# Cached key and value products of the sample group as 32-row products on four column quarters

## What is computed

```
s = jnp.einsum('bqhd,bld->bqhl', qi, ki)           # indexer scores, top 256 of 2056 keys
logits = jnp.einsum('bqhd,bqkhd->bqhk', q, ks) * HEAD_DIM ** -0.5
p = softmax(logits over the selected keys)
ya = jnp.einsum('bqhk,bqkhd->bqhd', p, vs)         # 8 heads of 64
```

## Time and profile before

| | us |
|---|---|
| median of 3 runs | 1352.07 |
| the runs | 1347.96, 1352.07, 1356.02 |
| span of the profiled execution | 1348.8 |
| TensorE busy | 1272.5 (94%) |
| VectorE busy | 712.7 (53%) |
| ScalarE busy | 251.3 (19%) |
| mean granted TensorE clock | 0.954 |

### The profile page before, as it was taken

One profiled execution on the slowest core, in us unless ns is written; L12 is line 12 of the kernel. 1 busy time (PEld: TensorE's weight loads), 2 busy tenths in 40 slices (PEclk: granted clock), 3 DMA queues, 4 the chain that ended last, 5 costly groups with the idle time before them and its releaser, 6 DMA issues.

```text
span 1348.8 us, 18080 instructions
## 1 busy us (share of the span) xinstructions
PE 1272.5 (94%) x5538; PEld 672.8 (50%) x5538; DVE 712.7 (53%) x1949; ACT 251.3 (19%) x576; POOL 66.3 (5%) x110
## 2 busy tenths in 40 slices
PE   6999999998998989999989999999999989999996
PEld 3643454564444655555446434554644456545642
DVE  3434488857885433433234336888488843423421
ACT  3023210113011113212210231110131011222121
POOL 2100000010100000001001000000101000000000
PEclk9999999998999897999998999999999989699898
DMA  7423045462567663644344011544626586255410
GB/s 234 136 83 125 1 154 185 164 222 88 195 219 251 227 210 110 200 155 146 98 130 168 1 63 63 191 166 138 231 96 218 189 306 224 96 192 193 138 34 37
DMA packets 111546, 204.88 MB, mean 152 GB/s; under 512 B 14439, under 2 KB 31062, under 8 KB 111474
## 3 DMA queue, kind: packets, MB, share of 16 engines
q1 hardware_dynamic: 96178, 149.73, 33.9%
q0 software_dynamic: 15296, 54.19, 11.6%
HBM read 193.85 MB, written 10.14 MB: 151 GB/s over the span
## 4 chain that ended last, share of the span: by engine, by line
PE 88%; DVE 4%; DMA 3%; issue 2%; ACT 2%; SPq 0%; POOL 0%; PEldq 0%; DVEq 0%; ACTq 0%; POOLq 0%
PE bank L1236 33%; PE bank L1270 11%; PE bank L1326 9%; PE bank L1568 7%; PE bank L1217 6%; PE bank L1387 4%; PE bank L1396 4%; PE bank L1474 3%; PE bank L1460 2%; DMA wr<-in_w_in_dram 2%; PE bank L1531 2%; PE bank L1486 2%; DVE sh L881 1%; PE bank L1250 1%; PE bank L1305 1%
## 5 line engine op out<-in xcount | busy, mean ns | idle before, releaser
L1236 PE MATMUL bank<-wr,ht 128*128 128x512 f32 (+3 forms) x1184 | 444.6, 532 | 4.0 <-ACT za L636 1.9
L1236 PEld LDWEIGHTS bank<-wr,ht 128*128 128x128 f32 (+1 forms) x1184 | 208.3, 190 | 227.4 <-issue 216.9
L835 DVE TENSOR_SCALAR_CACHE_REDUCE r<-r,sel_i 64x2112 bf16<-64x2112 f32 (+3 forms) x248 | 253.2, 1058 | 4.4
L1270 PE MATMUL bank<-pg,r 128*64 128x256 f32 x1024 | 164.6, 391 | 3.8 <-DMA pg<-in_cache_k_dram 3.0
L1270 PEld LDWEIGHTS bank<-pg,r 128*64 128x64 f32 x1024 | 107.5, 139 | 60.1 <-issue 16.3
L1326 PE MATMUL bank<-pg,rs 128*64 128x512 f32 x512 | 128.4, 611 | 0.0
L1568 PE MATMUL bank<-wr,ht 128*128 128x512 f32 x256 | 110.8, 593 | 0.0
L1217 PE MATMUL bank<-wr,ht 128*64 128x256 f32 (+1 forms) x640 | 76.3, 395 | 4.8 <-DMA wr<-in_w_in_dram 4.2
L1568 PEld LDWEIGHTS bank<-wr,ht 128*128 128x128 f32 x256 | 48.3, 190 | 60.1 <-issue 60.1
L1326 PEld LDWEIGHTS bank<-pg,rs 128*64 128x64 f32 x512 | 43.2, 138 | 64.2 <-issue 59.1
L932 DVE CUSTOM_DVE_ANT_0 r<-bank,r 128x256 f32<-128x256 f32 (+2 forms) x48 | 26.7, 557 | 90.4 <-PE bank L1387 90.4
(11 more groups left out here) (231 smaller groups left out, 1200.9 us busy)
## 6 DMA issues: line engine op xcount, KB each, us to landing
pg<-in_cache_k_dram SPq DMA_DIRECT2D x256, 256.0 KB, 4.2
pg<-in_cache_v_dram SPq DMA_DIRECT2D x256, 256.0 KB, 4.3
wr<-in_w_in_dram POOLq DMA_DIRECT2D x14, 2048.0 KB, 9.8
wr<-in_w_out_dram POOLq DMA_DIRECT2D x4, 2048.0 KB, 10.9
r<-in_x_prompt_dram SPq DMA_DIRECT2D x8, 512.0 KB, 6.0
sh<-in_cache_kidx_dram SPq DMA_DIRECT2D x128, 32.0 KB, 2.2
gr<-in_cache_kidx_dram SPq DMA_DIRECT2D x128, 32.0 KB, 2.1
out_dram<-vt POOLq DMA_DIRECT2D x8, 256.0 KB, 2.3
```

Of the source, the lines that this page charges most:

```text
L835: ins = nc.vector.tensor_scalar(junk[i][0:m, 0:part.shape[1]], part, sc, None, ALU.is_ge, ALU.add, accum_out=CNT[0:m, i:i + 1])
L1236: mm = pe.matmul(b[0:m, 0:w], HT[:, k, rt * P:rt * P + m], W[n % 2][:, k, 0:w], start=(k == 0), stop=(k == KC - 1))
L1270: mm = pe.matmul(bk[par * NS:(par + 1) * NS, u * 256:(u + 1) * 256], qc, two[:, :, c, :], start=(c == 0), stop=(c == NC4 - 1), skip_group_ ...
```

## The change

A key step's 64-row products become 32-row products. The rows of a sample are split into two halves of the heads, e = 0 (heads 0 to 3) and 1 (heads 4 to 7). For half e only the chunks 2e and 2e + 1 aren't zero, so each half takes 2 products instead of 4, each with 32 weight columns, at column quarter `r0` = 64 `par` + 32 e of the array. The loops are turned round: for each pair of groups (one of each sample) both are waited for, and the four quarters take turns. `v_step` likewise makes 32 rows x 256 columns (the channels of the half's own heads), 16 products instead of 8, in turns over the quarters. TensorE's wait and increment at the end of `k_step` go away: `act_full` no longer counts key steps (`act_fulls`), and ScalarE waits for `group_used`. `OWN` is 4 heads wide, `TARGET` has 16 columns per half, `turn_out` has 2 products of 32 columns per pair instead of 4 of 16, and the copy to `HT` is two instructions.

```
-    add("ownhead", ((pr[:, None] // TQ) % H == np.arange(H)[None]) * 1.0)
+    add("ownhead", ((pr[:, None] // TQ) % (H // 2) == np.arange(H // 2)[None]) * 1.0)
...
+    half = (pr // HW) % 2
+    add("target", np.concatenate([own_row & (half == e)[:, None] for e in range(2)], 1) * 1.0)
...
+ACT_FULL = {u: sum(v[0] != "s" for v in ACT_USES[:n + 1]) for n, u in enumerate(ACT_USES)}
...
             def copy_logits(l, hf, n):
...
-                b = full(l, "s", p, j)
+                act.wait_ge(group_used, (l * 4 + hf * 2) * GPP + 4 * (n + 1))
+                b = act_banks[act_no(l, "s", p, j) % 2]
...
-                    nc.vector.scalar_tensor_tensor(OD[hf][i].rearrange("p (h d) -> p h d", h=H),
-                                                   pv_banks[i][:, :].rearrange("p (h d) -> p h d", h=H), ESUM[:, 2 * i:2 * i + 1],
-                                                   OWN.unsqueeze(2).to_broadcast([P, H, HD]), ALU.mult, ALU.mult)\
+                    nc.vector.scalar_tensor_tensor(OD[hf][i].rearrange("p (h d) -> p h d", h=H // 2),
+                                                   pv_banks[i][:, 0:DP].rearrange("p (h d) -> p h d", h=H // 2),
+                                                   ESUM[:, 2 * i:2 * i + 1],
+                                                   OWN.unsqueeze(2).to_broadcast([P, H // 2, HD]), ALU.mult, ALU.mult)\
...
                 for u in range(2):
+                    two = []
                     for par in range(2):
-                        s0 = group(l, hf, 0, n)
-                        two = pg[:, s0 * DA:(s0 + 2) * DA].rearrange("p (e c n) -> p e c n", e=2, c=NC4)
-                        for c in range(NC4):
-                            qc = QBX[:, c, (2 * p + par) * NS:(2 * p + par + 1) * NS]
-                            mm = pe.matmul(bk[par * NS:(par + 1) * NS, u * 256:(u + 1) * 256], qc, two[:, :, c, :],
-                                           start=(c == 0), stop=(c == NC4 - 1), skip_group_check=True)
-                        mm.then_inc(group_used, 1)
-                        n += 1
-                pe.wait_ge(group_used, (l * 4 + hf * 2) * GPP + n)
-                pe.sem_inc(act_full, 1)
+                        s0 = group(l, hf, 0, n + par)
+                        two.append(pg[:, s0 * DA:(s0 + 2) * DA].rearrange("p (e c n) -> p e c n", e=2, c=NC4))
+                    for k in range(2):
+                        for par in range(2):
+                            for e in range(2):
+                                r0, q0 = par * NS + e * HW, (2 * p + par) * NS + e * HW
+                                mm = pe.matmul(bk[r0:r0 + HW, u * 256:(u + 1) * 256], QBX[:, 2 * e + k, q0:q0 + HW],
+                                               two[par][:, :, 2 * e + k, :], start=(k == 0), stop=(k == 1),
+                                               tile_position=(0, r0), skip_group_check=True)
+                            if k == 1:
+                                mm.then_inc(group_used, 1)
+                    n += 2
...
                     for u in range(2):
-                        for par in range(2):
-                            s0 = group(l, hf, 1, n)
-                            for e in range(2):
-                                c0 = (u * 2 + e) * P + par * NS
-                                mm = pe.matmul(acc[par * NS:(par + 1) * NS, :], RS[k % 2][:, c0:c0 + NS], PG[s0 + e],
-                                               start=(j == 0 and u == 0 and e == 0), stop=False, skip_group_check=True)
-                            mm.then_inc(group_used, 1)
-                            n += 1
+                        s0 = [group(l, hf, 1, n + par) for par in range(2)]
+                        for e in range(2):
+                            for par in range(2):
+                                for g in range(2):
+                                    r0 = par * NS + g * HW
+                                    c0 = (u * 2 + e) * P + r0
+                                    mm = pe.matmul(acc[r0:r0 + HW, 0:DP], RS[k % 2][:, c0:c0 + HW],
+                                                   PG[s0[par] + e][:, g * DP:(g + 1) * DP],
+                                                   start=(j == 0 and u == 0 and e == 0), stop=False,
+                                                   tile_position=(0, r0), skip_group_check=True)
+                                if e == 1:
+                                    mm.then_inc(group_used, 1)
+                        n += 2
...
-                    for c in range(NC4):
-                        mm = pe.matmul(bk[:, c * 32 + i * 16:c * 32 + (i + 1) * 16], OD[hf][i][:, c * P:(c + 1) * P], TARGET,
+                    for c in range(2):
+                        mm = pe.matmul(bk[:, i * 64 + c * 32:i * 64 + (c + 1) * 32], OD[hf][i][:, c * P:(c + 1) * P], TARGET,
                                        start=True, stop=True)
```

More of the change, by code:

```diff
@@ L326, in build @@
         SHC = [sh[:, i * PAST:(i + 1) * PAST] for i in range(2)]
-        OD = [[SP_[0], SP_[1]], [sh[:, i * PAST:i * PAST + DA] for i in range(2)]]
+        OD = [[SP_[0][:, 0:DP], SP_[1][:, 0:DP]], [sh[:, i * PAST:i * PAST + DP] for i in range(2)]]
         SHN = [sh[:, 2 * PAST + i * NS:2 * PAST + (i + 1) * NS] for i in range(2)]
@@ L520, in load_w @@
                     last = ("z", CHUNKS[iw][0], RTO[4]) if iw < len(CHUNKS) else ("o", RTO[4], iw - len(CHUNKS))
-                    pool.wait_ge(act_full, act_no(lw, *last) + 1)
+                    pool.wait_ge(act_full, act_fulls(lw, *last))
                 if i < len(CHUNKS):
@@ L612, in full @@
             def full(l, *u):
-                n = act_no(l, *u)
-                act.wait_ge(act_full, n + 1)
-                return act_banks[n % 2]
+                act.wait_ge(act_full, act_fulls(l, *u))
+                return act_banks[act_no(l, *u) % 2]
             def evac_z(l, name, rt):
@@ L1084, in _ @@
                     if s[0] == "queries":
-                        dve.wait_ge(act_full, act_no(l, "pi", 3, H - 1) + 1)
+                        dve.wait_ge(act_full, act_fulls(l, "pi", 3, H - 1))
                         then(nc.vector.memset(r2[:, :], 0.0))
@@ L1282, in new_keys @@
                         b = 4 * hf + 2 * i + par
-                        for c in range(NC4):
-                            mm = pe.matmul(bk[par * NS:(par + 1) * NS, i * NS:(i + 1) * NS], QBX[:, c, b * NS:(b + 1) * NS],
-                                           KNT[:, c, :], start=(c == 0), stop=(c == NC4 - 1), skip_group_check=True)
+                        for k in range(2):
+                            for e in range(2):
+                                r0, q0 = par * NS + e * HW, b * NS + e * HW
+                                mm = pe.matmul(bk[r0:r0 + HW, i * NS:(i + 1) * NS], QBX[:, 2 * e + k, q0:q0 + HW],
+                                               KNT[:, 2 * e + k, :], start=(k == 0), stop=(k == 1),
+                                               tile_position=(0, r0), skip_group_check=True)
                 mm.then_inc(act_full, 1)
@@ L1321, in v_step @@
                     for u in range(2):
-                        for par in range(2):
-                            s0 = group(l, hf, 1, n)
-                            for e in range(2):
-                                c0 = (u * 2 + e) * P + par * NS
-                                mm = pe.matmul(acc[par * NS:(par + 1) * NS, :], RS[k % 2][:, c0:c0 + NS], PG[s0 + e],
-                                               start=(j == 0 and u == 0 and e == 0), stop=False, skip_group_check=True)
-                            mm.then_inc(group_used, 1)
-                            n += 1
+                        s0 = [group(l, hf, 1, n + par) for par in range(2)]
+                        for e in range(2):
+                            for par in range(2):
[5 more added lines that the diff above has]
+                                                   start=(j == 0 and u == 0 and e == 0), stop=False,
+                                                   tile_position=(0, r0), skip_group_check=True)
+                                if e == 1:
+                                    mm.then_inc(group_used, 1)
+                        n += 2
                 else:
                     for par in range(2):
-                        mm = pe.matmul(acc[par * NS:(par + 1) * NS, :], RS[k % 2][0:NS, par * NS:(par + 1) * NS],
-                                       V[0:NS, ST, :], start=False, stop=True, skip_group_check=True)
+                        for g in range(2):
+                            r0 = par * NS + g * HW
+                            mm = pe.matmul(acc[r0:r0 + HW, 0:DP], RS[k % 2][0:NS, r0:r0 + HW],
+                                           V[0:NS, ST, g * DP:(g + 1) * DP], start=False, stop=True,
+                                           tile_position=(0, r0), skip_group_check=True)
                     mm.then_inc(out_full, 1)
```

14 lines of the change are left out of this document (10 added, 4 removed).

## The result

| | before | after |
|---|---|---|
| median of the runs, same chip | 1354.05 | 1307.09 |
| the runs from, to | 1347.96, 1358.6 | 1294.72, 1313.29 |
| span of the profiled execution | 1348.8 | 1310.6 |
| mean granted TensorE clock in it | 0.954 | 0.882 |

The kernel is faster: the ratio is 0.9643, 95% interval 0.9583 to 0.9704, or 48 us. The forecast was 82 us less, 1270, with a range that began at 1256 and ended at 1300. So the sign was right and over two fifths of the expected gain is missing. Where is it? In what follows, two runs of `own_keys` and one of `own_mask_filled` that fell in a slower state are in the medians but not in the ratios.

A forecast was written before the change was run, and what follows sets the result against it. TensorE was taken to bound the kernel, with VectorE and then the page ring behind it. Gains of 44.4 us per layer, less 3.4 for the clock, over two layers: 1352.1 - 82 = 1270, range 1256 to 1300.

The forecast's parts named there:

- The step: A key or value step of 16 products over four column quarters takes 2.05 us; ideal 1.77.
- Both rivals against packing: Key and value steps: two products at a time, 3.65 us, 1330 (chance 0.10); one at a time, 7.06, 1515 (0.05).
- The estimate of 2.3: A step at the Trainium skill's 3.07 times speedup: 7.06/3.07 = 2.3 us, making the sum 4 us higher.
- Items 1 and 2: First 8 key steps, then mask to `turn_out`: gains of 14.9 and 11.7 us per layer, both capped by VectorE.
- some 7 us: In the first key stretch, some 7 us turn into a wait of TensorE on VectorE.
- Item 3: `turn_out` has 4 products instead of 8: 1.94 becomes 1.0, gain 0.9 us per layer.
- Items 4 and 6: Second-half key steps gain 7.5 us per layer; value steps between heads 7.4, plus 1.4 for the two last steps.
- products 1.0: Term for a pair's products in the page ring's cycle at the second-half key steps, 1.0 us within 7.7.
- Off goes 3.4 for the clock: Allowance of 3.4 us per layer for TensorE's idle time, taken off the gain of 44.4.
- near 1.00 in the late heads: Sign to look for: granted TensorE clock near 1.00 in the late heads; wrong if heads run at 0.50.
- the clock stays low among the heads: Rival, chance 0.13: half clock makes head work 1.4 times as long, 12 us per layer over two thirds of steps: 1294.

The follow-up runs named there:

- own_keys: The changed kernel with only key steps waiting for one group at a time, value steps still for pairs: 1286.27, ratio 0.9430 to the kernel before.
- own_mask_filled: `own_groups` with an idle product ahead of each of the ten mask products before the second half's heads: 1276.82, ratio 0.9438 to the kernel before.
- own_groups: The changed kernel with key and value steps waiting for one group, issuing its products and freeing it before the next: 1270.67, ratio 0.9385 to the kernel before.
- pair_wait: `own_groups` with its product order kept but both groups of a pair waited for before the first product: 1306.09, ratio 0.9637 to the kernel before.
- values_only: The changed kernel with key steps, new keys and `act_full` bookkeeping from the kernel before: 1334.59, ratio 0.9884 to the kernel before.
- filled: The changed kernel with idle products on constants ahead of second-half key and value steps: 1296.26, ratio 0.9579 to the kernel before.

## Why the prediction was right and wrong

- **The step.** 2.05 was forecast, 1.93 measured: 0.16 over the ideal 1.77, where the forecast had added 0.28. Both rivals against packing (two or one at a time, 3.65 or 7.06) fell with this row. The estimate of 2.3 from the Trainium skill ("TensorE: Matmul & The Clock Gate", Measured speedup vs the span model), by its factor of 3.07, was too high: this trace has 7.06/1.93 = 3.66. The four products that the Trainium skill times there are packed in rows of the array, these in columns.
- **Items 1 and 2.** 128.1 and 112.4 forecast, 128.7 and 113.1 measured. TensorE idles 5.0 and 1.9 us at the keys' transposes, both put down to VectorE, the "some 7 us" of item 1. Here mechanism and size were right:

```profile
285.27 0.65 PE L1266 MATMUL bank<-cst,zb 64*128 64x64 f32 x4 [5.00 <-DVE zb L837]
```

- **Item 3.** 0.9 for `turn_out` was its length at full clock. At the half level it took 1.92 in place of 1.94: no gain.
- **Items 4 and 6** are sound as far as they count pages, and wrong in "products 1.0". The second-half key steps end at 443.96, 453.23 and 462.25, so 9.3 and 9.0 apart, not 7.7:

```profile
442.02 1.94 PE L1289 MATMUL bank<-pg,r 128*32 128x256 f32 x16 [1.51 <-DMA pg<-in_cache_k_dram]
443.89 0.79 PE L1417 MATMUL bank<-kt,qt 64*128 64x128 f32 x2
...
447.09 1.94 PE L1289 MATMUL bank<-pg,r 128*32 128x256 f32 x16
451.30 1.93 PE L1289 MATMUL bank<-pg,r 128*32 128x256 f32 x16 [2.27 <-DMA pg<-in_cache_k_dram]
```

  One period is 1.94 + 2.27 + 1.93 + 3.2 of head work (443.89 to 447.09) = 9.3. At full clock the products are 1.07 each, and a piece of head work such as L1417's 0.79 is 0.49 in `own_groups`. The chain of waits shows the ring's cycle itself:

```profile
442.02 1.99 PE bank L1289 x16
...
445.72 5.44 DMA pg<-in_cache_k_dram
451.16 0.14 issue
451.30 1.99 PE bank L1289 x16
```

  Products 1.99, then 1.7 until the reload of the last group starts (444.01 to 445.72), 5.44 for it, 0.14: 9.3, against 1.0 + (0.2 + 1.1) + 5.4 = 7.7 forecast. So 1.0 of the 1.6 over it are the products at the half level, 0.4 are SP's issues and 0.14 TensorE's start. The products stand inside the cycle, between a landing and the next issue, so the half clock lengthens the cycle. That the longer cycle in turn keeps the clock low is argued, not shown.
- **The step that failed** is the line "Off goes 3.4 for the clock". 3.4 us per layer stood there; what came over the forecast without it was 24 per layer (48.3/2), the greater part of it in stretches at a low clock. The prediction saw the cause, "TensorE now idles ... 2 to 3 us in each ring-bound period", and gave it a price without working one out. So items 4 and 6 kept "products 1.0", where 1.93 to 1.99 were measured, and the sign "near 1.00 in the late heads" failed with 0.89 and 0.70. Part of the low level comes from ahead of these stretches: from 387.4 to 406.3, with waits for pages and for VectorE, TensorE was busy 8.2 of 18.9 us and the clock was 0.64.
- **The rival that happened** is "the clock stays low among the heads". Its mechanism was right, its place was not: it priced the heads alone and left out the second-half key steps, where 15.8 of the 48.3 lie. Its 12 us per layer for the heads is near the 14 measured in part by luck: it reckoned with the half level over two thirds of them, and 22% and 60% were measured. With the key steps' 16, known only from the result, its time would be 1310. The clock fell at about 441 us, behind one burst of 1.07 us between waits of 2.39 and 1.51. The Trainium skill ("TensorE: Matmul & The Clock Gate", HAM oscillation — how this bites in real kernels) has bursts shorter than the DMA wait between them lose the clock; for the fall this trace agrees. It doesn't explain that the clock then stayed at 0.50 up to the value steps: between the waits of 2.27 and 2.02 us TensorE worked for 7.0 us.
- **What the forecast had in the wrong kernel.** Its 1270 is the time of `own_groups`, which is a coincidence: the prediction reckoned with waits for pairs. In item 4 the prediction counted what waiting for a pair does to the page ring and found nothing (7.7 as before). It did not ask what it does to TensorE's busy time in the ring-bound stretches.

How much of the 36 us between the two orders of waiting is the clock alone? For the heads' stretch the windows of the changed kernel, `pair_wait` and `values_only` can be laid on a line: (us at half clock, us in all) are (16, 70.6), (52, 86.3), (38, 78.9), (35, 79.0), (18, 70.5), the first number being 2 x (1 - clock) x length. The line of least squares has a slope of 0.44 and gives 63.0 at no half-clock time, near the forecast's 64.6. That argues that in the heads the loss is the clock's. It is a fit of five windows, not a run, and a longer wait could also be what lowers the clock. By the idle products some 18 of the 36 us, give or take 11, come back with the clock; the other 17, give or take 6, could be waiting as such, or clock that `filled` did not restore. That split stays open. The runs' own spread goes the same way: the four runs of the changed kernel, at clocks 0.893, 0.887, 0.882 and 0.881, took 1294.72, 1301.74, 1312.44 and 1313.29.

## What to carry to other kernels

When products are packed into quarters of the array, first ask which stretches were bound by TensorE and which by a transfer: in the first kind the step's saving arrives until the next engine caps it (143.0 to 128.7, where VectorE did), in the second the packed burst is short, the gap behind it long, and here the clock fell to half for all work around it. Wait for each buffer right ahead of the products that use it, even if that leaves half of the quarters idle: here this cost 0.03 us per step where data was ready and gave 2.5% of the kernel where it was late. In a forecast, price a ring-bound stretch at both clock levels, its products and the head work alike, and take the high level only where the gaps are short.

## What the runs showed that was not expected

- Four products of 256 columns on two quarters take 1.06 us, as long as eight on four quarters, 1.07; yet a step in the order 0, 1, 0, 1, 2, 3, 2, 3 takes 1.96 in all, with 1.93 for the order that goes round all four. The start of the second group overlaps the first to that extent.
- 22 idle products per layer cost some 9 us over the kernel where the clock was high anyway, and won about 18, give or take 11, where it was low. They are a remedy, but a worse one than moving the wait.
- The clock level alone is no measure of loss: 0.58 and, with idle products, 0.76 in the first heads gave the same 29.6 and 29.8 us, while in the value steps among the heads each us at half clock went with about 0.4 us more.
